# Turning gathered expert rows on VectorE in 32x32 blocks, with the scaling on ScalarE

## What is computed

```python
logits = xt @ w_router + b_router                # 32 experts
top_vals, top_idx = lax.top_k(logits, 4)
gates = softmax(top_vals)
order = argsort(top_idx.reshape(-1)); xs = xt[order // 4]
h = ragged_dot(xs, w_gate_up, group_sizes) + b_gate_up[e_sorted]
glu = minimum(h[:, ::2], 7.0); lin = clip(h[:, 1::2], -7.0, 7.0)
act = glu * sigmoid(1.702 * glu) * (lin + 1.0)
y = ragged_dot(act, w_down, group_sizes) + b_down[e_sorted]
out = segment_sum(y * gates, tok, 1024)
```

## Time and profile before

| | |
|---|---|
| median of 3 runs | 2710.2 us (2705.48 to 2710.97) |
| span of the profiled execution | 2705.4 us |
| expert stage | from about 1091 us to the end |
| PE busy | 2638.0 us (98%) |
| DVE busy | 1091.5 us (40%) |
| ACT busy | 627.4 us (23%) |
| mean granted clock of TensorE | 0.990 |

### The profile page before, as it was taken

The page is one execution under the profiler, slowest core; times in us unless marked ns, Lnnn a source line. Parts: engine busy times, 40 slices in busy tenths (PEclk is TensorE's granted clock), DMA queues, the critical chain, the costliest instruction groups (busy, mean ns, idle before and its releaser), DMA issues.

```text
span 2705.4 us, 49571 instructions
## 1 busy us (share of the span) xinstructions
PE 2638.0 (98%) x17206; PEld 2118.7 (78%) x17207; DVE 1091.5 (40%) x2701; ACT 627.4 (23%) x1386; POOL 379.9 (14%) x391
## 2 busy tenths in 40 slices
PE   9999999999999998999999999999999999999997
PEld 8455556666477774999999999998878787878785
DVE  1111145554212324433333344344455454545455
ACT  0333355553011112011111111111212121221212
POOL 0100022221000001111111111111111111112111
PEclk9999999999999998999999999999999999999998
DMA  8111243232300002765667677787888888888885
GB/s 293 47 51 54 64 151 90 79 116 92 129 1 9 31 31 103 303 209 194 221 218 254 225 276 260 269 274 264 318 299 319 301 310 306 312 297 312 300 310 202
DMA packets 108856, 533.95 MB, mean 197 GB/s; under 512 B 24290, under 2 KB 59042, under 8 KB 84208
## 3 DMA queue, kind: packets, MB, share of 16 engines
q1 hardware_dynamic: 88016, 498.99, 50.2%
q0 software_dynamic: 20768, 33.97, 5.7%
HBM read 506.64 MB, written 60.52 MB: 210 GB/s over the span
## 4 chain that ended last, share of the span: by engine, by line
PE 92%; DVE 3%; issue 2%; DMA 2%; ACT 1%; DVEq 1%; POOL 0%; ACTq 0%; POOLq 0%
PE bank L1376 45%; PE wide L1376 9%; PE wide L1836 9%; PE wide L1804 9%; PE bank L1426 8%; PE bank L1369 4%; PE wide L1500 2%; PE bank L1556 2%; PE bank L1760 2%; PE wide L1517 1%; DMA d_sum<-y_sb,sidx 1%; PE wide L1369 1%; DVE biased L2060 1%; DVE prob_t L2071 1%; ACT prob L1151 0%
## 5 line engine op out<-in xcount | busy, mean ns | idle before, releaser
L1376 PE MATMUL bank<-xe_t,slot 128*128 128x128 f32 (+4 forms) x8192 | 1025.2, 287 | 12.3 <-issue 11.2
L1376 PEld LDWEIGHTS bank<-xe_t,slot 128*128 128x128 f32 x8192 | 1014.5, 192 | 14.1 <-issue 13.7
L2336 DVE TENSOR_SCALAR glu<-bank,b_gu 128x256 f32<-128x256 f32 x256 | 123.8, 484 | 657.2 <-PE bank L1376 657.1
L1317 ACT ACTIVATE sig<-glu 128x256 f32<-128x256 f32 x256 | 106.7, 417 | 837.8 <-DVE glu L2336 835.5
L1836 PE MATMUL wide<-slot,act_t 128*128 128x512 f32 x608 | 267.8, 593 | 1.0 <-DVE act_t L2348 1.0
L1804 PE MATMUL wide<-act_t,slot 128*128 128x144 f32 (+3 forms) x1664 | 235.5, 302 | 0.0
L1804 PEld LDWEIGHTS wide<-act_t,slot 128*128 128x128 f32 x1664 | 231.8, 190 | 0.0
L1426 PE MATMUL bank<-w_in,xt 128*128 128x512 f32 (+1 forms) x512 | 217.6, 575 | 1.6 <-DVEq L1978 1.6
L1836 PEld LDWEIGHTS wide<-slot,act_t 128*128 128x128 f32 x608 | 112.5, 190 | 128.8 <-issue 126.2
L1334 ACT ACTIVATE y_t<-wide,b_dn 128x256 f32<-128x256 f32 x248 | 102.0, 471 | 421.2 <-PE wide L1836 212.9
L955 POOL DMA_INDIRECT xg<-d_xn,gidx x66 | 66.6, 1009 | 862.8 <-DVE gidx L2290 814.0
(11 more groups left out here) (302 smaller groups left out, 2455.6 us busy)
## 6 DMA issues: line engine op xcount, KB each, us to landing
slot<-in_w_gu SPq DMA_DIRECT2D x128, 2048.0 KB, 8.8
slot<-in_w_dn SPq DMA_DIRECT2D x64, 2048.0 KB, 7.7
w_in<-in_w_in SPq DMA_DIRECT2D x1, 6144.0 KB, 25.3
w_mem_k<-in_w_mem_kv SPq DMA_DIRECT2D x4, 1024.0 KB, 11.0
w_mem_v<-in_w_mem_kv SPq DMA_DIRECT2D x1, 4096.0 KB, 20.6
x_sb<-in_x SPq DMA_DIRECT2D x8, 512.0 KB, 3.3
cneg<-d_cneg SPq DMA_DIRECT2D x8, 512.0 KB, 6.6
d_vw<-mix_out SPq DMA_DIRECT2D x16, 256.0 KB, 2.2
```

The source lines that it names most:

```text
L1317: ac.activation(sig[m % 2][:, :], glu[m % 2][:, :], ACT.Sigmoid, scale=1.702).then_inc(e_sig, 1)
L1376: m = pe.matmul(dst, l, r_, start=(k == 0), stop=(k == n - 1))
L2336: ve.tensor_scalar(glu[b][:, :], pp[b][:, 0:CAP], b_gu[:, bass.ds(e * 2 * KD + 2 * m, 1)], 7.0, ALU.add, ALU.min).then_inc(e_glu, 1)
```

## The change

TensorE no longer turns the gathered rows, except for the first item. VectorE does: `rows_turned` makes 32 transposes of one 32-partition group into another, each of eight 32x32 blocks, from xg into a new buffer xs. Four of them stand behind each block m = 3 to 7 of `step`, and twelve more at its end. ScalarE then scales xs by g_ffn into xe_t with eight copies (its new `rows_in`), which stand in its program between y_t 1 and y_t 2, and signals e_xt.

```diff
@@ scalar engine
+            def rows_in(i):
+
+                ac.wait_ge(e_turned, i)
+                for k in range(KD):
+                    ac.activation(xe_t[:, k, :], xs[:, k, :], ACT.Copy, scale=g_ffn[:, k:k + 1])
+                ac.drain().then_inc(e_xt, 1)
...
                     if m % 4 == 3:
                         ac.sem_inc(e_w[4 + m // 4].free, 1)
+                    if m == 1:
+                        rows_in(i + 1)
                 ac.drain().then_inc(e_yt, 1)
@@ tensor engine
                 e_gate_up(i, 3, 8, w)
-                e_turn_in(i + 1, (0, 1), later)
                 if w == P:
-                    e_rows_down(i, lambda: e_turn_in(i + 1, (2, 3), later))
+                    e_rows_down(i)
                     look_ahead()
                     return
                 e_down_first(i, w)
-                e_turn_in(i + 1, (2, 3), later)
                 e_down(i, (1, 3, 4, 5), w)
@@ vector engine
+            QR = 32
+            QUARTERS = [(hb, g, q) for hb in range(2) for g in range(P // QR) for q in range(P // QR)]
+
+            def rows_turned(i, n0, n1):
+
+                if n0 == 0:
+                    ve.wait_ge(e_xg, 32 * (i + 1))
+                for hb, g, q in QUARTERS[n0:n1]:
+                    ve.transpose(xs[q * QR:(q + 1) * QR, :, hb * P + g * QR:hb * P + (g + 1) * QR],
+                                 xg[g * QR:(g + 1) * QR, hb, :].rearrange("p (k c) -> p k c", k=KD)[:, :, q * QR:(q + 1) * QR])
+                if n1 == len(QUARTERS):
+                    ve.drain().then_inc(e_turned, 1)
...
             hots(1, expert_at(1))
+            ve.wait_ge(s_st, 16 * (NT + 1))
...
+                    if m >= 3 and not last:
+                        rows_turned(i + 1, 4 * (m - 3), 4 * (m - 2))
+                ve.drain()
+                if not last:
+                    rows_turned(i + 1, 20, 32)
                     hots(i + 2, nxt)
```

More of the change, by code:

```diff
@@ L277, in build @@
         xg = r("xg", [P, 2, D])
+        xs = Region(15, 23)("xs", [P, KD, CAP])
         r = Region(47, 63)
@@ L447, in index_use, with turn_in_use @@
         def index_use(i):
-            return e_pt[0].base + 3 * i + 1
-        def turn_in_use(b, i, k):
-            return e_pt[b].base + (3 * i + 1 + k if b == 0 else 2 * i + k)
+            return e_pt[0].base + (1 if isinstance(i, int) and i == 0 else 3 + i)
+        def turn_in_use(b, k):
+            return e_pt[b].base + (1 + k if b == 0 else k)
         def rows_use(b, i, k, beyond=False):
@@ L580, in build @@
         e_dn = [Handoff(sem, f"e_dn{b}") for b in range(2)]
+        e_turned = sem("e_turned")
         e_xt, e_glu, e_sig, e_act, e_yt = sem("e_xt"), sem("e_glu"), sem("e_sig"), sem("e_act"), sem("e_yt")
@@ L1359, in ac_further, with ac_first @@
                 rows_back(i, 16)
-            further_blocks(ac, ac_further, lambda: ac.sem_inc(e_y.full, 1), lambda: squares(range(NT), 3))
+            def ac_first():
+                ac.sem_inc(e_y.full, 1)
+                rows_in(E)
+            further_blocks(ac, ac_further, ac_first, lambda: squares(range(NT), 3))
         @block.tensor
@@ L1747, in e_index, with first_turn_in @@
                           lambda: tokens(1, 1).then_inc(e_pt[0].full, 1))
-            def e_turn_in(i, groups, n=None):
-                pe.wait_ge(e_xg, 32 * (i + 1))
-                for g in groups:
+            def first_turn_in():
+                pe.wait_ge(e_xg, 32)
+                for g in range(4):
                     b, k = g % 2, g // 2 + 1
[L1754 to L1763, removed]
+                    pe.wait_ge(e_pt[b].free, turn_in_use(b, k))
+                    for j in range(4):
+                        c = 2 * g + j // 2
+                        m = pe.transpose(pt[b][:, j * P:(j + 1) * P], xg[:, j % 2, c * P:(c + 1) * P], ident)
+                    m.then_inc(e_pt[b].full, 1)
             def rows_free(b, i, k, beyond=False):
@@ L1826, in e_down, with e_rows_down @@
                     down(i, m, w)
-            def e_rows_down(i, turn_in):
+            def e_rows_down(i):
                 for hd in range(2):
@@ L1845, in e_rows_down @@
                             .then_inc(s, 1)
-                    if hd == 0:
-                        turn_in()
             def rows_in(i):
@@ L1909, in item @@
                 with pe.If_lt(at, 1):
-                    e_turn_in(0, range(4))
+                    first_turn_in()
                 whole(i, i - 1, w, n_before, later, look_ahead)
@@ L2295, in indices, with first_copies @@
                 ve.drain()
-            def x_copies(i, groups=range(4)):
-                for g in groups:
+            def first_copies():
+                for g in range(4):
                     b, k = g % 2, g // 2 + 1
-                    ve.wait_ge(e_pt[b].full, turn_in_use(b, i, k))
+                    ve.wait_ge(e_pt[b].full, turn_in_use(b, k))
                     scaled(xe_t[:, 2 * g:2 * g + 2, :], pt[b][:, :], g_ffn[:, 2 * g:2 * g + 2], 2, CAP)\
                         .then_inc(e_pt[b].free, 1)
-                if groups[-1] == 3:
-                    ve.drain().then_inc(e_xt, 1)
+                ve.drain().then_inc(e_xt, 1)
+            QR = 32
[8 more added lines that the diff above has]
+                    ve.drain().then_inc(e_turned, 1)
             def hots(i, e):
@@ L2326, in _ @@
             ve.drain().then_inc(r_gate, 1)
-            x_copies(0)
+            first_copies()
             hots(1, expert_at(1))
+            ve.wait_ge(s_st, 16 * (NT + 1))
             def step(i, e, last=False):
@@ L2469, in _ @@
             normed(y_sb[:, 0, :], last_rows[:, :], rstd_l[:, 1:2])
-            x_copies(E, (2, 3))
             def more_hots():
+                ve.wait_ge(f_out, 16 * NT)
+                rows_turned(E, 0, len(QUARTERS))
                 hots(E + 1, expert_at(E + 1))
```

## The result

| | before | after |
|---|---|---|
| median | 2709.05 us (2705.48 to 2710.97, 4 runs) | 2791.43 us (2790.47 to 2793.12, 4 runs) |
| span of the profiled execution | 2705.4 us | 2788.8 us |
| mean granted clock of TensorE | 0.990 | 0.977 |

The change makes the kernel slower, by the ratio 1.0307 (95% interval 1.0293 to 1.0322): 82 us, where I had forecast 41. It lies inside the stated range (2680 to 2830 us). The direction and the reason hold, and the size does not.

A forecast was written before the change was run, and what follows sets the result against it. TensorE was taken to bound the kernel (busy 2638 of 2705.4 us). Terms 27 + 15 - 1 - 7 - 1 = +33 us, plus 8 for clock falls, on 2710.2 gave 2751 us; range 2680 to 2830.

The forecast's parts named there:

- The turns cost more than they give back: Narrow items (at most 128 rows): transposes and copies delay the next gate-up, +1.5 us at each of 18 handovers, +27 us.
- The spacing s: Time from one VectorE transpose's start to the next: taken as 0.47 us, with 0.33 and 0.77 as ends.
- the prediction's own sum: Narrow handover: next gate-up at t + 1.5 + 32s, t being gate-up's end, against 15.05 us before; TensorE idles about 2.4 us.
- The wait for y_t 3: Items at 144 columns: idle of about 3 us before down's block 6; +2.6 us on each of six items, +15 us.
- I allow five such falls, +8 us: TensorE's granted clock drops to half after idle handovers; five drops at 1.7 us each allowed for.
- all 24 handovers: Rival: the clock falls at every one, 41 us in place of 8, so 2784 us, up to 2820; chance 0.13.
- few falls: Main forecast: s between 0.43 and 0.53 and the clock seldom at half, 2715 to 2810 us; chance 0.48.
- I take no wait: Narrow items, behind block m = 3: gathered rows land at 2267.0, about when act_t ends at 2266.83, so no delay.
- the signs that I had named for a wrong chain of times: First transpose waits for the gather, or TensorE stalls in gate-up for a bank: chain wrong even if the total fits.
- the mechanism among the rivals: Rival: w_dn refills run nearer the gather, so it lands later; 3 us later gives 2823 us; chance 0.05.
- No stall in row-form down: Narrow items: block 7's act_t ends at t + 5.6, wanted only at t + 6.0, so down doesn't stall.
- VectorE at some 75% in narrow items: Sign to look for: VectorE's busy share over narrow items, about half of such an item before the change.

The follow-up runs named there:

- Experiment 2: Changed kernel with the second sixteen transposes put behind block 7 and made only for items of over 128 rows; 2720.57 us, ratio 1.0046 to the kernel before.
- Experiment 3: Changed kernel with ScalarE's eight copies behind y_t 3 instead of y_t 1, which also moves a w_dn refill; 2737.75 us, ratio 1.0113 to the kernel before.
- experiment 4: Changed kernel with the same 32 transposes reordered, the two halves of rows innermost; 2722.81 us, ratio 1.0052 to the kernel before.
- experiment 1: Changed kernel with two unread 512-column matmuls on TensorE ahead of its wait for e_xt in narrow items; 2781.08 us, ratio 1.027 to the kernel before.
- experiment 5: Changed kernel with w_dn slot 4 released before ScalarE's copies, the copies left in place; 2769.74 us, ratio 1.0233 to the kernel before.

## Why the prediction was right, and where it was wrong

**The turns cost more than they give back: right.** The spacing s was 0.45 us, and I had taken 0.47. Eight copies take 3.30 us in place of 3.0. The handover wait is 2.3 us, near the forecast ("about 2.4 us, released by ScalarE's xe_t"), and the narrow items lose 25.1 us by it, against +27. Part of this closeness is luck: with the measured s and copies the prediction's own sum gives 1.8 + 14.4 - 14.2 = 2.0 us, and 1.90 was measured where the signal of block 3 was on time; the other 0.39 us is that late signal, which no term had. Experiment 2 shows that it is the transposes: with sixteen fewer the wait is zero.

**The wait for y_t 3: right in place, a little large.** 2.96 us stands ahead of down's block 6 in all six items at 144, against "about 3 us". It brings +11.7 us with the wait for act_t, against +15. Experiment 3 shows that it hangs on the copies' place. At 160 columns the same wait is 1.32 us in three items, where I took 0 to -0.4; the wider handovers together were -8.7 against -8.

**The clock: the step that failed.** "I allow five such falls, +8 us" is the term that was mis-sized. There were 15 in 18 narrow handovers and one in each of six items at 144: 24.3 + 11.4 = 36 us. I had priced one fall rightly (1.7 us; it is 1.62) and even had its rival, all 24 handovers, at 0.13 and 2784 us. What was measured is that rival's case, 21 of 24, though the time also falls inside the 2715 to 2810 of "few falls". The argument against it was that the trace before showed one fall after 2.2 us and the new waits were hardly longer; but waits of 2.3 us were enough in most cases and not in all. The trace before had more to say: four of its own handovers have waits of 2.4 to 3.3 us, and the clock was at half behind two of them, at 1236.15 and 1540.37, and up behind those at 1368.52 and 1850.02. Its windows behind the first and the last:

```profile
1238.00:1240.00 2.00, 2.00 (x8) 0.50 0.94 401
...
1851.00:1853.00 2.00, 2.00 (x20) 1.00 1.11 475
```

Half of 24 would have been 12 falls and 20 us. In experiment 4 the wait is 1.4 us at most and the clock stays up. The Trainium skill, "TensorE: Matmul & The Clock Gate", section "HAM oscillation", describes a kernel in which a wait in each tile drops the clock each time, with longer waits than here; the 15 falls and experiment 1, where useless work in the gap kept the clock up, agree with it.

**The gather: "I take no wait" was wrong.** Nine narrow waits of 0.9 to 1.6 us make 10.4 us. That the first transpose waits, and that TensorE is stalled in gate-up for a bank (by up to 0.6 us in these items), were the signs that I had named for a wrong chain of times. I had the mechanism among the rivals (the w_dn refills asked for nearer the gather), at 0.05, and by it named the right cause: experiment 5 takes the waits away, all but one, by moving one refill. What I missed is that the act_t chain left so little slack, and that ScalarE's delay put the two requests within 0.95 us where they had been spread over 5.79.

**No stall in row-form down: nearly.** Nine waits of up to 0.7 us, 4.7 us in all, stand there, in the nine items that also waited for the gather.

**VectorE at some 75% in narrow items: right in effect.** It never waits from block 4 on. Of the 83 us, the 5.7 us of rest are not followed to their end, nor is the cause of the 0.39 us of late signal inside most of the handover waits.

**Why the two errors did not add up singly.** With the clock at full speed at narrow handovers the gather waits are 36.8 us and not 16.9 (experiment 1). And with the refills apart, experiment 5 gained 22 us and not 10. So neither number is what its removal brings.

## What to carry to other kernels

When an engine off the bound takes over work, count how far it ends behind the bound's own handover, and then ask what a stall of two microseconds does to the bound's clock. Here a stall of 2.3 us cost 2.3 and, at 14 of 17 handovers, another 1.6, and a reordering that took a microsecond off the helper gave 69 us over 18 handovers and six wider ones. Two losses at one place hide each other, so an experiment on one alone tells too little; and before moving a step on the helper engine, look what else its program releases behind it (here a 2 MB refill).

## What the runs showed of the hardware

- Transposes of 32 partitions by 256 f32 elements take 436 ns and start 0.45 us apart when each writes another group of partitions than the last, and 0.39 us apart on the mean when every second one stays in its group (that one starts 0.37 us after the first and takes 0.39).
- The clock fell at 14 of 17 handovers with 2.3 us idle in the kernel after, at none of four such in experiment 3, at six of twelve with 1.9 us there, and at none with 1.4 us (experiment 4). In the kernel after it fell between 0.2 us before and 1.3 us after the work had come back. A wait of 1.90 us did not do it at 2071.78 in experiment 3, while one of 1.90 us at 1916.06 in the kernel after was followed by 9.03 us for the same 64 records.
- With two loads of 2 MB asked for within 0.95 us ahead of it, the gather landed in 6.8 us in the median (experiment 1), late enough for 1.7 us of wait at block 3; with the loads spread over 6.87 us, in 4.8 us, and all but one of the waits were gone (experiment 5).
- The 0.45 us by which the signal of block 3 is late stays open.
